# Streaming a tile of 256 columns through the matmul in eight interleaved blocks of 32, with the weights placed 64 bytes further on

## The reference, cut to what matters

```python
# first block
x = x + parallel_mixer(rmsnorm(x, norm_mix_g), ...)      # mLSTM and latent attention, then w_out
x = x + memory_cross_attention(rmsnorm(x, norm_x_g), ...)
x = x + square(relu(rmsnorm(x, norm_ffn_g) @ w_ff1)) @ w_ff2          # 1024 -> 4096 -> 1024
# second block, on the 16 meta rows and the 256 rows of x
h = h + 0.5 * swiglu(rmsnorm(h, ffn1_norm), w_gate, w_up, w_down)     # 1024 -> 2816 -> 1024
u = rmsnorm(h, mix_norm); ... = split(u @ w_in)
mixed = sigmoid(gate_a) * (ya @ w_branch_att) + sigmoid(gate_b) * (yb @ w_branch_gla)
h = h + mixed @ w_out
h = h + 0.5 * swiglu(rmsnorm(h, ffn2_norm), w_gate, w_up, w_down)
return rmsnorm(h, final_norm)[:, 16:]
```

## The kernel before, in words

| stage | product | tiles streamed | groups x blocks x feature tiles | matmuls (x3) |
|---|---|---|---|---|
| ff1a, ff1b | `w_ff1`, two halves | `U` | 4 x 4 x 8 each | 384 each |
| ff2a, ff2b | `w_ff2`, two halves | `H` | 2 x 4 x 16 each | 384 each |
| out2 | `w_out_2` | `H` | 2 x 4 x 8 | 192 |
| sw2 | gate and up of swiglu 2 | `U` | 11 x 4 x 8 | 1056 |
| dn2 | down of swiglu 2 | `H` | 2 x 4 x 22 | 528 |

## Time and profile before

### The profile page before, as it was taken

The page is one execution under the profiler, slowest core; times in us unless marked ns, Lnnn a source line. Parts: engine busy times, 40 slices in busy tenths (PEclk is TensorE's granted clock), DMA queues, the critical chain, the costliest instruction groups (busy, mean ns, idle before and its releaser), DMA issues.

```text
span 911.4 us, 18458 instructions
## 1 busy us (share of the span) xinstructions
PE 896.9 (98%) x7415; PEld 880.6 (97%) x7415; DVE 642.1 (70%) x1108; ACT 525.5 (58%) x869; POOL 4.7 (1%) x11
## 2 busy tenths in 40 slices
PE   8999999999999999999999999999999999999996
PEld 7997999999999999999999999999999999999996
DVE  6999888777557666666675547768669877677553
ACT  6897876676336655444444435545775664544452
POOL 1000000000000000000000000000000000000000
PEclk9999999999999999999999999999999999999999
DMA  9742335255765666555556565554425556665641
GB/s 307 239 166 97 139 121 181 93 186 193 251 189 177 200 204 185 171 173 171 181 174 199 168 177 161 158 169 130 148 70 186 186 185 196 201 194 195 212 138 47
DMA packets 110613, 157.63 MB, mean 173 GB/s; under 512 B 9917, under 2 KB 61249, under 8 KB 110401
## 3 DMA queue, kind: packets, MB, share of 16 engines
q1 hardware_dynamic: 109776, 155.19, 53.2%
q10 hardware_dynamic: 576, 0.73, 0.2%
q0 software_dynamic: 176, 0.53, 0.2%
HBM read 155.37 MB, written 1.05 MB: 172 GB/s over the span
## 4 chain that ended last, share of the span: by engine, by line
PE 90%; DVE 6%; ACT 2%; issue 1%; DMA 1%; SPq 0%; DVEq 0%; ACTq 0%
PE ps L1044 28%; PE ps L1046 28%; PE ps L1045 27%; DVE wl L1817 2%; PE ps L1127 1%; ACT wh L1383 1%; PE ps L1091 1%; DMA X<-d_x 1%; DVE S L2222 1%; PE ps L1301 0%; PE ps L1321 0%; DVE S L2068 0%; PE ps L1259 0%; DVE X L1981 0%; PE ps L1281 0%
## 5 line engine op out<-in xcount | busy, mean ns | idle before, releaser
L1817 DVE TENSOR_TENSOR wl<-raw,wh 128x1024 fp32r<-128x1024 f32 (+2 forms) x291 | 346.2, 1212 | 191.4 <-ACT wh L1383 191.2
L1383 ACT ACTIVATE wh<-raw 128x1024 fp32r<-128x1024 f32 (+2 forms) x291 | 298.2, 1046 | 186.8 <-PE ps L1046 186.3
L1044 PE MATMUL ps<-U,wh 128*128 128x256 f32 (+2 forms) x1392 | 397.5, 286 | 2.3 <-DVE wl L1817 2.3
L1046 PE MATMUL ps<-U,wl 128*128 128x256 f32 (+2 forms) x1392 | 390.9, 281 | 0.0
L1045 PE MATMUL ps<-UL,wh 128*128 128x256 f32 (+2 forms) x1392 | 390.4, 280 | 0.0
L1044 PEld LDWEIGHTS ps<-U,wh 128*128 128x128 f32 (+1 forms) x1392 | 262.2, 188 | 5.3 <-DVE wl L1817 3.2
L1045 PEld LDWEIGHTS ps<-UL,wh 128*128 128x128 f32 (+1 forms) x1392 | 262.5, 189 | 1.6 <-issue 1.0
L1046 PEld LDWEIGHTS ps<-U,wl 128*128 128x128 f32 (+1 forms) x1392 | 262.0, 188 | 0.0
L1044 PE MATMUL ps<-H,wh 128*128 128x256 f32 (+1 forms) x736 | 207.4, 282 | 0.1
L1046 PE MATMUL ps<-H,wl 128*128 128x256 f32 (+1 forms) x736 | 205.4, 279 | 0.0
L1045 PE MATMUL ps<-HLO,wh 128*128 128x256 f32 (+1 forms) x736 | 205.1, 279 | 0.0
(11 more groups left out here) (340 smaller groups left out, 784.2 us busy)
## 6 DMA issues: line engine op xcount, KB each, us to landing
raw<-w_ff SPq DMA_DIRECT2D x64, 512.0 KB, 4.5
raw<-ffn_w_gate SPq DMA_DIRECT2D x88, 256.0 KB, 3.6
raw<-ffn_w_up SPq DMA_DIRECT2D x88, 256.0 KB, 4.5
raw<-ffn_w_down SPq DMA_DIRECT2D x44, 512.0 KB, 4.6
raw<-w_in SPq DMA_DIRECT2D x40, 512.0 KB, 4.0
raw<-w_out SPq DMA_DIRECT2D x16, 512.0 KB, 3.6
raw<-wkv_x SPq DMA_DIRECT2D x8, 512.0 KB, 4.2
raw<-w_in SPq DMA_DIRECT2D x9, 256.0 KB, 3.0
```

Source lines behind the costliest of these rows:

```text
L1044: e.matmul(out, sh, xh, start=(i == 0 and n == 0), stop=False)
L1046: mm = e.matmul(out, sl, xh, start=False, stop=(over and n == nk - 1))
L1383: e.activation(wh, raw, ACT.Copy).then_inc(*up("w_hi", v))
L1817: lo = e.tensor_tensor(wl, raw, wh.bitcast(F32), ALU.subtract)
```

## The change

It touches the stages in a new list `HALVES`, the seven of the table above. The moving tile and the output of their matmuls are described in another order: `by_halves` cuts 256 columns into eight blocks of 32 and goes through them as 0, 4, 1, 5, 2, 6, 3, 7. The output is addressed in the same order, so that each column's sum ends where it was. And `first_columns` begins the weights of these stages 16 columns (64 bytes) later, at columns 16 and 528, so that a weight block begins 128 bytes past its tile's start, counted by remainders of 256.

No instruction is added, removed or put elsewhere: every engine issues the same operations in the same order with the same waits. The ScalarE and VectorE instructions that write `wh` and `wl` keep their size and write 64 bytes further on. The matmul instruction has a form 128x4x2x32 in place of 128x256.

```diff
+HALVES = ("ff1a", "ff1b", "ff2a", "ff2b", "out2", "sw2", "dn2")
+
+
 def first_columns(name, g, i):
 
 
     ks, width = GEMM[name].units(g)[i], GEMM[name].width(g)
+    if name in HALVES:
+        return [16 + n * width for n in range(len(ks))]
     skew = {"sw1": 0, "dn1": 0, "in2": g == 2, "gvr": g, "gab": 1}.get(name)
...
+def by_halves(a):
+
+    return a.rearrange("p (q g c) -> p g q c", q=2, g=4)
...
             out = ps[0:m, 0:xh.shape[-1]]
+            if name in HALVES:
+                xh, xl, out = by_halves(xh), by_halves(xl), by_halves(out)
             sh, sl = wh[:, n, off:off + m], wl[:, n, off:off + m]
```

## The result

The changed kernel took 934.2 us (median of four runs, 932.87 to 935.81), the kernel before 912.0 beside it (four runs, 910.78 to 912.97). The ratio is 1.0236, with a 95% interval of 1.0203 to 1.0268: 22.2 us slower. Forecast were 912.1 us with a range of 906 to 928, so the time lies outside the range.

What follows compares the result with a forecast made beforehand. The prediction took the seven stages to be bound by TensorE alone, at 113.3 ns per matmul. Its terms summed 0 + 0 + 0 + 0, leaving the profiled 911.4 us, forecast as 912.1 us, range 906 to 928.

Steps and rivals of the forecast that it cites:

- Step (a): Seven stages: the new block order keeps stream and load apart; at most 5.3 us gained, taken as nothing.
- second rival: Seven stages reach the load's own pace, 111.7 ns per matmul: 5.3 us less, 906.8 us; chance 0.28.
- Step (b): Seven stages' matmuls: cost of eight pieces, from nothing to 12.4 ns per matmul, 41 us; taken as nothing.
- slow rhythm: Pace of 117.9 ns per matmul seen in `uv` and `o`; as a sign, 45.3 us for 384 matmuls in ff2a.
- fourth rival: Jumps cost by themselves, through non-contiguous PSUM access or in reading: up to 12.4 ns per matmul, 953 us; chance 0.08.
- Step (c): Weights 64 bytes further on: no cost if the new order keeps stream and load apart, otherwise up to 15.2 us.
- third rival: Every matmul of the seven stages falls to 117.9 ns under the new alignment: 15.2 us more, 927 us; chance 0.26.
- good rhythm: The better of two paces at equal addresses, 113.3 ns per matmul, in which the seven stages were said to run.
- Step (d): ScalarE and VectorE splits writing at another offset: even some 50 ns more each would be hidden; taken as nothing.
- The starts 384 apart: Deciding sign in ff2a: 43.5 us no change, 42.9 load's pace, 45.3 or 48.3 for the two slower cases.
- costly jumps: Case that jumps between pieces cost by themselves: 48.3 us for 384 matmuls in ff2a; chance 0.08.
- seven equal amounts: Sign of jumps costing by themselves: the seven stages' pace off by a multiple of these, without two rhythms.

Runs made afterwards that it cites:

- e8: Kernel before, but the second and third matmul of each block of three stream only 128 of 256 columns: 912.9 us, ratio 0.9963.
- e12: Kernel before, but the second and third weight load of each block take only 32 of 128 columns: 912.4 us, ratio 0.9968.
- e14: Changed kernel with the weights 256 bytes past the tile's start, the same position by remainders of 256: 930.9 us, ratio 1.0168.
- e2: Changed kernel with only the new order of tile and output, weights left at 64 bytes: 929.5 us, ratio 1.0163.
- e20: Changed kernel with all three weight loads of a block cut to one column, except each tile's first and last: 927.0 us, ratio 1.0135.
- e6: Changed kernel with four blocks of 64 columns, order 0, 2, 1, 3, in place of eight of 32: 929.8 us, ratio 1.0145.
- e13: Kernel before, but ff2a, ff2b, out2 and dn2 stream high and low tile as one 512-column matmul, two loads per block: 920.9 us, ratio 1.0067.
- e7: Changed kernel with sixteen blocks of 16 columns in place of eight of 32: 933.3 us, ratio 1.0183.
- e3: Changed kernel with the output written in plain order, the tile still read in blocks: 934.8 us, ratio 1.0221.
- e4: Changed kernel with the tile read in plain order, the output still written in blocks: 930.6 us, ratio 1.0175.
- e1: Changed kernel with only the weights' new place, tile and output in plain order: 929.3 us, ratio 1.0160.
- e10: Changed kernel with block order 0, 2, 4, 6, 1, 3, 5, 7 and weights at 64 bytes: 934.7 us, ratio 1.0221.
- e19: Changed kernel in plain order, all three weight loads of a block cut to one column, except each tile's first and last: 914.3 us, ratio 1.0001.

## Why the prediction was wrong

**What bounds the kernel.** Right. The seven stages are TensorE's alone, and a change of pace came through to the end one for one: 22.1 us by the paces, 22.2 by the medians.

**Step (a), the gain of the order, taken as nothing.** The term was right, the reason only in part: e8 puts loads beside shorter streams at 113.33 ns on average, not at the 112 of the earlier trace rows or the 111.7 that I carried, and I did not know that the stream needs the same 113.33 by itself (e12). So the second rival, with its chance of 0.28, had nothing to give. That the order helps by keeping stream and load 128 bytes apart is contradicted by e14.

**Step (b), the cost of the eight pieces.** This is the first step that failed: "They lie between the two, nearer to the slow rhythm, so I take nothing." The step costs 5.5 ns at the old placement (e2, 18.1 us) and 4.5 with no loads beside it (e20). The earlier trace rows could not price it, either way: its pieces have 128 columns, 512 bytes, four times as long as those of the change, and e6 shows no cost of pieces of 256 bytes. Nor is its 5.3 ns shown to be a cost of jumps: one matmul of 512 columns with a single jump takes 234 to 235 ns in e13. So I took nothing from a row of another form, with the slow rhythm as the reason, and both were no evidence. Its upper end, 1.8 ns per jump, had the wrong form as well: e6 and e7 show no cost per jump. Of the fourth rival the mechanism "or in reading" is right, "PSUM access" is wrong (e3, e4), and its 12.4 ns were twice too much.

**Step (c), the weights 64 bytes further on.** The second: "It has no cost of its own if (a) holds." The premise was half right (nothing to gain) and the conclusion wrong. The placement alone costs 5.3 ns, 17.7 us (e1), against my bound of 4.6 ns and 15.2 us. The third rival had the mechanism of this half, stream and load in each other's way, and the place, every matmul of the seven stages, though not the pace: 118.67 is another than the 117.8 of the slow rhythm. Its argument, that the good rhythm is the exception and any other arrangement may lose it, held for each of the seven orders and places tried with three whole loads per block (after, e1, e2, e6, e7, e10, e14), and e13's ff1b shows the good rhythm lost without any other arrangement. By these runs it deserved more than 0.26.

**The size.** 4.6 ns was read off `o` and `uv`, which run in the slow rhythm at the good placement; that price of the rhythm was right (e13's ff1b, 4.5 ns), but it is not what the change costs. Both costs together are 6.7 ns, 22.1 us. So even the third rival's time, 927, is 7 us short, and the range, which ended just above it, missed: it took the two costs as alternatives, though the change makes both edits, and (c) and (b) should have been summed at their upper ends.

**Step (d).** Right: the splits kept their durations, and TensorE's idle time ahead of its 1392 matmuls on `U` in the first of the three lines went only from 2.3 to 3.1 us by the pages.

**The signs I named.** The starts 384 apart gave 46.08 us, between "slow rhythm" (45.3, where e13's ff1b lies with 45.23) and "costly jumps" (48.3). A rigid 120.00 looked like seven equal amounts, as I had said jumps would show; e7 shows that this sign was none.

**What stays open.** What makes reading in pieces below 256 bytes cost about 4 ns when hardly anything is loaded; why e2 and e14 stay 1 ns below the rigid 120.00 of e3, e7 and e10; what decides in which rhythm a stage runs, in `uv` and `o` and in e13's ff1b, at the same addresses, and whether the 117.8 to 118.0 of e20 has to do with it. Blocks at the old placement without loads were not run, nor the kernel before without any.

## What to carry to other kernels

Before you rearrange addresses for a faster stream, find both floors: shorten the streams, then the loads, and see whether the pace moves. Where neither does, as here, another place of the weights can only lose. A rigid pace over hundreds of matmuls is no sign of a floor: 113.33 and 120.00 ns were equally rigid. When two edits each have a cost that you can only bound, put both upper ends into the range together, and do not price pieces of 128 bytes from a row with pieces of 512. And where the same code at the same addresses shows two paces, compare stage by stage over several traces before you put a pace down to an edit.

## What the runs showed of the hardware that I had not expected

- A float32r matmul follows the one before after its columns at 2.4 GHz and 6.7 ns: 60.0 ns for 128 columns (e8), 113.33 for 256 (e12). With 272 columns it is 3.6 to 3.8 ns more than this gives (123.6, 123.8 after). Whole loads of 128 weight columns come to 113.33 ns on average when a third of the streaming is gone (e8).
- The same code at the same addresses has two rhythms, 113.3 and 117.8 ns, and a stage can keep the slow one for 384 matmuls (e13's ff1b against before).
- The place of the weights relative to the tile is worth 5.3 ns of 113 (e1), and this is gone, to within 1 ns, with hardly any loads (e19).
- Reading a tile in pieces of 128 bytes costs about 4 ns with hardly any loads (e20 against e19); pieces of 256 bytes cost nothing that shows beside whole loads (e6 against e1); writing the output in pieces of 128 bytes adds nothing at 118.67 and 120.00 ns (e4 against e1, e3 against after).
